# Summing scaled expert rows on TensorE: two 512-column identity matmuls in place of eight 128-column transposes

## The reference

```
x   = layer_norm(ALPHA * x + token_mix(x))
out = layer_norm(ALPHA * x + peer(x))

peer, per token t (8 heads, 16 experts of 16384 for each head):
  act = gelu(einsum('td,tkd->tk', x, u[expert])) * gate      # 128 experts a token
  out = einsum('tk,tkd->td', act, v[expert])                 # rows of 1024 values
```

## Time and profile before

| | us |
|---|---|
| median of the runs (783.46, 783.79, 947.14) | 783.79 |
| the profiled execution's own time | 783.51 |
| its span, first to last instruction | 781.8 |
| PE, PEld busy | 557.8, 463.9 |
| DVE, ACT, POOL busy | 545.8, 456.9, 283.5 |
| mean granted TensorE clock | 0.84 |
| mean DMA rate over the span | 385 GB/s |

### The profile page before, as it was taken

The page is one execution under the profiler, slowest core; times in us unless marked ns, Lnnn a source line. Parts: engine busy times, 40 slices in busy tenths (PEclk is TensorE's granted clock), DMA queues, the critical chain, the costliest instruction groups (busy, mean ns, idle before and its releaser), DMA issues.

```text
span 781.8 us, 10142 instructions
## 1 busy us (share of the span) xinstructions
PE 557.8 (71%) x3330; PEld 463.9 (59%) x3330; DVE 545.8 (70%) x1397; ACT 456.9 (58%) x818; POOL 283.5 (36%) x271
## 2 busy tenths in 40 slices
PE   9999999998988796658363647556565555465595
PEld 6485596876878696546363547445464555464541
DVE  1789479899935858485958486867676676767556
ACT  0244238877765766566656657565565656565633
POOL 0000014445534253525353434444434444434420
PEclk9999999999999898768777767676767877767799
DMA  8994029999999999999999999999999999999993
GB/s 309 387 394 181 27 88 388 424 419 420 420 416 421 422 420 421 420 422 421 422 421 420 420 423 421 422 421 420 420 421 423 422 422 422 422 422 422 422 419 158
DMA packets 49969, 301.09 MB, mean 385 GB/s; under 512 B 5236, under 2 KB 5892, under 8 KB 16520
## 3 DMA queue, kind: packets, MB, share of 16 engines
q0 software_dynamic: 37296, 268.45, 82.8%
q1 hardware_dynamic: 11448, 28.25, 9.6%
q10 hardware_dynamic: 1184, 3.88, 1.3%
HBM read 299.50 MB, written 1.06 MB: 384 GB/s over the span
## 4 chain that ended last, share of the span: by engine, by line
DMA 50%; PE 21%; DVE 15%; issue 7%; ACT 3%; POOL 2%; DVEq 0%; POOLq 0%; another core or an unknown queue 0%; ACTq 0%
DMA arena<-in_expert_uv,expert 47%; PE bank L544 7%; PE bank L725 5%; DMA arena<-in_expert_uv,last_rows 3%; DVE arena L1687 3%; PE bank L688 3%; PE bank L568 2%; ACT arena L1108 1%; PE bank L669 1%; POOL arena L504 1%; ACT weight L1098 1%; DVE big L1372 1%; PE bank L536 1%; DVE score L1672 1%; DVE picked L1673 1%
## 5 line engine op out<-in xcount | busy, mean ns | idle before, releaser
L725 PE MATMUL bank<-ident,arena 128*128 128x128 f32 x1920 | 306.9, 331 | 210.5 <-ACT arena L1108 209.4
L504 POOL DMA_INDIRECT arena<-in_expert_uv,expert x253 | 275.3, 1088 | 462.9 <-PE bank L725 228.8
L725 PEld LDWEIGHTS bank<-ident,arena 128*128 128x128 f32 x1920 | 285.4, 175 | 233.7 <-ACT arena L1108 230.3
L1687 DVE SCALAR_TENSOR_TENSOR arena<-x_sb,arena 128x1024 f32<-128x1024 f32 x256 | 307.2, 1224 | 162.5 <-DMA arena<-in_expert_uv,expert 145.6
L1108 ACT ACTIVATE arena<-arena,weight 128x1024 f32<-128x1024 f32 x240 | 257.0, 1138 | 2.2
L1093 ACT ACTIVATE gelu<-dots 128x4 f32<-128x4 f32 (+2 forms) x80 | 16.3, 204 | 212.7 <-DVE arena L1687 207.2
L1098 ACT ACTIVATE weight<-gelu,gate 128x1 f32<-128x1 f32 x256 | 56.4, 285 | 3.6
L544 PE MATMUL bank<-arena,x_t 128*128 128x512 f32 (+1 forms) x128 | 52.9, 565 | 0.1
L544 PEld LDWEIGHTS bank<-arena,x_t 128*128 128x128 f32 x128 | 24.5, 198 | 22.5 <-issue 20.3
L755 PE MATMUL bank<-arena,mid 128*128 128x512 f32 x58 | 27.0, 603 | 2.8 <-ACT mid L1105 1.6
L669 PE MATMUL bank<-arena,big 128*128 128x512 f32 x64 | 28.5, 592 | 0.0
(11 more groups left out here) (251 smaller groups left out, 551.5 us busy)
## 6 DMA issues: line engine op xcount, KB each, us to landing
arena<-in_w_in SPq DMA_DIRECT2D x5, 2048.0 KB, 21.1
arena<-in_w_out SPq DMA_DIRECT2D x2, 2048.0 KB, 19.2
arena<-in_expert_uv,expert POOLq DMA_INDIRECT x253
wq_homes<-in_peer_wq SPq DMA_DIRECT2D x2, 1024.0 KB, 20.3
mix<-in_peer_wq SPq DMA_DIRECT2D x2, 1024.0 KB, 10.7
big<-in_peer_wq SPq DMA_DIRECT2D x2, 1024.0 KB, 4.8
x_sb<-in_w_q ACTq DMA_DIRECT2D x1, 1024.0 KB, 9.7
ln_gb<-in_w_q ACTq DMA_DIRECT2D x1, 1024.0 KB, 12.1
```

Of the source, the lines that this page charges most:

```text
L504: pool.indirect_dma_start(out=arena[:, slot * SLOT:(slot + 1) * SLOT], out_offset=None, in_=expert_uv, in_offset=bass.IndirectOffsetOnAxis ...
L725: last = mm(banks[2 * tile + k // 4][:, (k % 4) * P:(k % 4 + 1) * P], lhsT=arena[:, at + k * P:at + (k + 1) * P], rhs=ident[:, :], is_tran ...
L1687: ins = stt(rows, x_rows[:, bass.ds(tile * D_MODEL, D_MODEL)], 1.0, rows, ALU.mult, ALU.mult, accum_out=dots[:, parity, j:j + 1])
```

## The change

`sum_slots` adds a scaled v row not by eight transposes but by two matmuls of 512 columns, with the identity as weights and the v row as the moving operand. The sum so lies in token rows, in banks 0 and 1 for tile 0 and 2 and 3 for tile 1. `copy_sum`, `sum_back`, `sum_t` and four semaphores go. The residual is added into the same banks: for tile 0 ahead of unit 7's sums, for tile 1 after the first group of unit 8, with `start=False`. The last unit's matmuls add into banks 2 and 3, and DVE reads the tile's own banks. Before tile 1's first group PE waits for banks 2 and 3 to be free of earlier jobs, where it waited for banks 4 to 7 after it.

```diff
                 for j in some:
                     pe.wait_ge(scaled_ready, u * SLOTS + j + 1)
-                    at = slots_of(u)[j] * SLOT + D_MODEL
-                    for k in range(KT):
-                        last = mm(banks[2 * tile + k // 4][:, (k % 4) * P:(k % 4 + 1) * P], lhsT=arena[:, at + k * P:at + (k + 1) * P],
-                                  rhs=ident[:, :], is_transpose=True, start=first_unit and j == 0 and k % 4 == 0,
-                                  stop=last_unit and j == SLOTS - 1, skip_group_check=True)
+                    for half in range(2):
+                        at = slots_of(u)[j] * SLOT + D_MODEL + half * 512
+                        last = mm(banks[2 * tile + half][:, :], lhsT=ident[:, :], rhs=arena[:, at:at + 512],
+                                  start=first_unit and j == 0, stop=last_unit and j == SLOTS - 1, skip_group_check=True)
                     last.then_inc(slot_used, 1)
-
-            def sum_back(t):
...
             def add_residual(t):
 
                 pe.wait_ge(alpha_ready, 1)
                 for half in range(2):
-                    mm(banks[SUM_BACK + half][:, :], lhsT=alpha_ident[:, :], rhs=x_sb[:, t, half * 512:(half + 1) * 512],
-                       start=True, stop=False, skip_group_check=True)
+                    mm(banks[2 * t + half][:, :], lhsT=alpha_ident[:, :], rhs=x_sb[:, t, half * 512:(half + 1) * 512],
+                       start=False, stop=False, skip_group_check=True)
...
-                        last = mm(banks[SUM_BACK + half][:, :], lhsT=diag[:, j % 8, :], rhs=arena[:, at:at + 512],
+                        last = mm(banks[2 * (TILES - 1) + half][:, :], lhsT=diag[:, j % 8, :], rhs=arena[:, at:at + 512],
...
-                    last.then_inc(half_back[0] if j == SLOTS - 1 else slot_used, 1)
+                    last.then_inc(last_sum_done if j == SLOTS - 1 else slot_used, 1)
...
+            add_residual(0)
             sum_slots(PEER_HEADS - 1, 0, last_unit=True)
+            for n in range(2, 4):
+                pe.wait_ge(bank_free[n], bank_uses[n])
             sum_group(PEER_HEADS, 0)
-            for n in range(4, PSUM_BANKS):
-                pe.wait_ge(bank_free[n], bank_uses[n])
-            add_residual(0)
-            sum_back(0)
+            add_residual(1)
             for g in range(1, 4):
                 sum_group(PEER_HEADS, g)
...
-            pe.wait_ge(sum_added, 2)
-            add_residual(1)
-            sum_last_slots(UNITS - 1, range(0, 4))
-            sum_back(1)
-            sum_last_slots(UNITS - 1, range(4, SLOTS))
+            sum_last_slots(UNITS - 1, range(SLOTS))
...
-                    if last and g == 1:
-                        copy_sum(TILES - 1)
-                    if isinstance(u, int) and u == PEER_HEADS and g == 0:
-                        copy_sum(0)
...
-                    dve.wait_ge(half_back[half], 1 + 2 * t)
-                    link(nc.vector.bn_stats(stats[:, 6 * half:6 * half + 6], banks[SUM_BACK + half][:, :]))
+                    if t == 0:
+                        dve.wait_ge(slot_used, PEER_HEADS * SLOTS)
+                    else:
+                        dve.wait_ge(last_sum_done, 1)
+                    link(nc.vector.bn_stats(stats[:, 6 * half:6 * half + 6], banks[2 * t + half][:, :]))
```

More of the change, by code:

```diff
@@ L171, in build_layer @@
         peer_q_t = view(mix, 0, PEER_QS, 2, P)
-        sum_t = view(mix, 1024, KT, P)
         iq_t, ik_t = view(mix, 2048, 2, SEQ), view(mix, 2560, SEQ)
@@ L272, in build_layer @@
         dots_ready, gelu_ready, weight_ready, diag_ready = (sem(n) for n in ("dots_ready", "gelu_ready", "weight_ready", "diag_ready"))
-        slot_used, scaled_ready, sum_added = (sem(n) for n in ("slot_used", "scaled_ready", "sum_added"))
-        sum_copied, half_back = ([sem(f"{n}{half}") for half in range(2)] for n in ("sum_copied", "half_back"))
-        SUM_BACK = 6
+        slot_used, scaled_ready, last_sum_done = (sem(n) for n in ("slot_used", "scaled_ready", "last_sum_done"))
         last_rows_ready, alpha_ready = sem("last_rows_ready"), sem("alpha_ready")
@@ L722, in sum_slots @@
                     pe.wait_ge(scaled_ready, u * SLOTS + j + 1)
-                    at = slots_of(u)[j] * SLOT + D_MODEL
-                    for k in range(KT):
-                        last = mm(banks[2 * tile + k // 4][:, (k % 4) * P:(k % 4 + 1) * P], lhsT=arena[:, at + k * P:at + (k + 1) * P],
-                                  rhs=ident[:, :], is_transpose=True, start=first_unit and j == 0 and k % 4 == 0,
-                                  stop=last_unit and j == SLOTS - 1, skip_group_check=True)
-                    last.then_inc(slot_used, 1)
-            def sum_back(t):
[L732 to L737, removed]
+                    for half in range(2):
+                        at = slots_of(u)[j] * SLOT + D_MODEL + half * 512
+                        last = mm(banks[2 * tile + half][:, :], lhsT=ident[:, :], rhs=arena[:, at:at + 512],
+                                  start=first_unit and j == 0, stop=last_unit and j == SLOTS - 1, skip_group_check=True)
+                    last.then_inc(slot_used, 1)
             def add_residual(t):
@@ L1109, in weigh_slots @@
                             scale=weight[:, parity, j:j + 1]).then_inc(scaled_ready, 1)
[L1111 to L1116, removed]
             def take_ln2(part):
@@ L1508, in add_last_values @@
                     at = slots_of(u)[j] * SLOT + D_MODEL + 512
-                    before = banks[SUM_BACK + 1][:, :] if n == 0 else x_sb[:, TILES - 1, halves[1]]
+                    before = banks[2 * (TILES - 1) + 1][:, :] if n == 0 else x_sb[:, TILES - 1, halves[1]]
                     link(stt(x_sb[:, TILES - 1, halves[1]], arena[:, at:at + 512], weight[:, 1, j:j + 1], before, ALU.mult, ALU.add))
@@ L1516, in centre @@
                 for half, part in enumerate(halves):
-                    source = banks[SUM_BACK + half][:, :] if summed and t + half < TILES else x_sb[:, t, part]
+                    source = banks[2 * t + half][:, :] if summed and t + half < TILES else x_sb[:, t, part]
                     ins = stt(x_sb[:, t, part], source, moments[:, 0:1], ln_gb[:, 0, part], ALU.subtract, ALU.mult)
                 link(ins)
-                if summed:
-                    dve.sem_inc(sum_added, 2)
             def spread(t, n, done):
```

## The result

The kernel after takes 796.69 us (median of 6 runs) against 783.68 us, ratio 1.0171 with a 95% interval of 1.0159 to 1.0182: 12.5 to 14.3 us slower. The ratio and its interval go by the undisturbed runs alone (one run of the kernel before took 947.14 us). The forecast was 796.5. The profiled span is 794.5 us, 12.7 more than before.

What follows compares the result with a forecast made beforehand. PE and DMA both bound the kernel to about 183 us, DMA alone afterwards. Span 781.8 + 12.7 of lost DMA time, 0 for the rest, gave 794.5, then 796.5 against the median; range 789 to 804.

Steps and rivals of the forecast that it cites:

- Price of a slot: PE's sum of one slot: four records at full clock, 1.717 us, which is 0.842 us more than before.
- Lateness at the 29th gather: At the gather issued at 183.36 us, PE is late by 19 slots x 0.842 = 16.0 us.
- Cover: DMA queue at 154.5 and 183.3 us, less a gather's start time: 3.3 us of PE lateness is free.
- Loss: DMA time lost through late early gathers: 16.0 - 3.3 = 12.7 us.
- The sign that I named: DMA share under 1 between 150 and 200 us, 12 to 13 us missing, and 1.01 from 202 on.
- L: Theory that only PE's lateness at releases of gathers up to the 29th costs, less 3.3 us covered by the queue.
- The second narrow place: Last release before query projections end, at 302.7 us: PE 30 us late, nothing lost, by only 4 us.
- Rival 3: A second DMA hole between 183 and 310 us, 3 to 8 us more deficit: 802; chance 19%.
- The rest of the edits: Dropped copies, transposes back and waits, moved residual matmuls, unchanged end: 0 us, bounds -1 and +2.
- One record per matmul: Rival 1: identity matmuls take one record each, a slot 0.86 us, PE never later: 783; chance 4%.
- More cover: Rival 2: the queue hides more of the early gathers' lateness, loss 6 to 9 us: 791; chance 16%.
- PE as the bound: Rival 4: at a lower clock PE's groups outlast DMA's 9.95 us to the end: 844; chance 3%.

Runs made afterwards that it cites:

- late halves left out: Kernel after, second 512 columns left out of the sum in 206 of 240 slots, units 2 to 14; 796.14 us, ratio 1.0149 to the kernel before.
- tile 1 alone in token rows: Kernel after's change for tile 1 only, tile 0 keeping transposes, copy and sum back; 783.82 us, ratio 0.9997 to the kernel before.
- unit 0's late halves left out: Kernel after, second 512 columns left out of the sum in slots 1 to 15 of unit 0; 784.35 us, ratio 0.9997 to the kernel before.
- the doubled loop: Kernel after, two more zero-weight matmuls of 512 columns for each slot of units 9 to 14; 890.53 us, ratio 1.1354 to the kernel before.

## Why the prediction was right, step by step

- *What bounds it*: right. DMA's share is 1.01 from 222 us on in both kernels.
- *Price of a slot*, four records and 1.717 us: right, 960 records, 3.44 us for two slots. Per column: a query projection is written as 16 matmuls of 128 columns and shows 32 records from 133.27 to 136.84 in PE's timeline above, so such a f32 matmul takes two records of 0.112 us; a transpose takes 0.109. That is a factor of 2.05. The Trainium skill, page "TensorE: Matmul & The Clock Gate", section Terms, says that the transpose mode is four times faster for FP32; the trace does not agree, with 2.05 for 128 columns and 1.717 against 0.875 us for a slot.
- *Lateness at the 29th gather*, 16.0 us: measured 15.8. PE had no idle time in the stretch, and DVE and ACT followed it (DVE is busy 26.13 of 33 us against 30.21). The 3 us that I held as a bound for them were not needed.
- *Cover*, 5.1 - 1.8 = 3.3 us: right to within the runs' resolution; 2.6 us of lateness are free, and 7.7 us cost 3.6 to 6.5.
- *Loss*, 12.7: span +12.7. That the profiled span meets it to the tenth is in part luck. By the bytes DMA lost 13.4 us; 1.3 us of it went before 150 us (382 GB/s against 405), where I had no loss; and the hole ended near 203 us and not 202. The sign that I named, the DMA share, shows only about half of the missing time. Against the medians' ratio, 12.5 to 14.3, it sits at the lower end. In five of the six kernels that lose DMA time early, the middle of the interval is 0.6 to 1.3 us above the sum by L, in the sixth (late halves left out) 1.0 below. DMA moved less for the same busy share in the hole (334 GB/s at 0.91), so a gather with few behind it may take longer than one that streams; no experiment isolates that.
- *The second narrow place*: the conclusion (no hole) was right, the sizes were not. I put PE 30 us late at the last query projections with 4 us of margin, and PE without idle until about 230 us. It had none until 357, and at that gather it was 25.9 us late (328.62 against 302.72). The term that I had too small is the time in which ACT paces PE's groups (6 us): PE took back 10. The narrowest point came a little sooner, at the gather issued at 319.86; DMA view from 113.3 to 319.8:

```profile
q0 software_dynamic: 10239, 74.63, 91.0%
...
arena<-in_expert_uv,expert POOLq DMA_INDIRECT x75, 16.3
```

  75 x 1.049 - 74.63 = 4.0 MB, 9.5 us queued, 7.7 us spare. Rival 3 was that far away, with twice the margin I gave it: the estimate of 6 us was some 4 too small, and the error happened to lie on the safe side.
- *The rest of the edits*, 0: right; tile 1 alone in token rows shows its new ending at 0 within 0.9 us, and unit 0's late halves left out shows all the rest at 0 within 1.1.
- *Rivals.* One record per matmul: out (960 records). More cover: out (DMA at 334 and 325 GB/s; 7.7 us of lateness already cost 3.6 or more). A second hole: out. PE as the bound: the clock in 300:700 rose to 0.91 instead of falling, and only the doubled loop, at 3.43 us a slot, makes PE the bound.

## What to carry to other kernels

When two engines are full in the same stretch, ask for the queue between them: count what is issued, subtract what has landed, take off the time from an issue to its first bytes, and you have the time by which the producer of free places may be late. As long as a buffer costs the engine less than it costs DMA, more work on it costs nothing behind a deep queue, and its full length, less the cover, behind a shallow one; here 143 us of new PE work cost 13, all by the first 19 slots. A form that drops copies and transposes can still lose, if it makes a step dearer in the one stretch where that step frees buffers.

## What the runs showed of the hardware

TensorE's clock and what kind of work holds it up. Between 300 and 700 us the kernel before works on transposes and the one with late halves left out on matmuls of 512 columns, both in bursts of a group about every 10 us, and the two are nearly equally busy: 214.41 and 215.28 us for the sums. By line, before and then with late halves left out:

```profile
300.00:700.00 400.00, 214.41 (x1260) 201.71 (x1261) 0.74 1.01 421
```

```profile
300.00:700.00 400.00, 215.28 (x321) 78.27 (x319) 0.76 1.01 421
```

The granted clock is 0.74 with transposes and 0.76 with matmuls; with full sums (306.34 us for the same groups) it is 0.91. So which of the two PE did made no difference to its clock here; the means lie between the two levels of 1.2 and 2.4 GHz. The Trainium skill, page "TensorE: Matmul & The Clock Gate", section "PE-mode transpose", says that the full clock doesn't engage for transpose mode, which doesn't count as PE-busy in the same way. It says so beside bf16 figures; for these f32 transposes the trace does not agree: 0.74 against 0.76, and 1.00 in 150:183 with groups of transposes between the matmuls.

An identity as weights brings no discount: 960 records for 480 matmuls, as for any f32 matmul here.
